# Feed-forward units of a split-precision decoder kernel: from 512-column and 256-column matmuls to 256-column matmuls throughout

## What is computed

```python
def _swiglu(x, w_gate, w_up, w_down):
    return (jax.nn.silu(x @ w_gate) * (x @ w_up)) @ w_down

for l in range(DEPTH):                      # DEPTH = 2
    x = _layer_norm(DN_ALPHA * x + 0.5 * _swiglu(x, ffn1...), ln1_g[l], ln1_b[l])
    x = _layer_norm(DN_ALPHA * x + _hybrid_mixer(x, ...), ln2_g[l], ln2_b[l])
    x = _layer_norm(DN_ALPHA * x + 0.5 * _swiglu(x, ffn2...), ln3_g[l], ln3_b[l])
```

## Time and profile before

| | |
|---|---|
| median of 3 runs | 1286.24 us (1286.09 to 1286.31) |
| the profiled execution's own time | 1286.24 us |
| its span | 1283.9 us |
| TensorE (PE) busy | 1272.0 us, 99% |
| PE weight loads (PEld) busy | 1143.4 us, 89% |
| DVE busy | 911.8 us, 71% |
| ACT busy | 642.0 us, 50% |
| granted TensorE clock, mean | 0.999 |

### The profile page before, as it was taken

One profiled execution on the slowest core, in us unless ns is written; L12 is line 12 of the kernel. 1 busy time (PEld: TensorE's weight loads), 2 busy tenths in 40 slices (PEclk: granted clock), 3 DMA queues, 4 the chain that ended last, 5 costly groups with the idle time before them and its releaser, 6 DMA issues.

```text
span 1283.9 us, 18456 instructions
## 1 busy us (share of the span) xinstructions
PE 1272.0 (99%) x7905; PEld 1143.4 (89%) x7905; DVE 911.8 (71%) x1106; ACT 642.0 (50%) x662; POOL 68.8 (5%) x59
## 2 busy tenths in 40 slices
PE   8999999999999999999999999999999999999997
PEld 7888889998999988888888888899989998888886
DVE  6566669898675787665686666799977756866665
ACT  5444445694544354444454444466836454544441
POOL 0299000000000000000000000000000000000000
PEclk9999999999999999999999999999999999999999
DMA  8855647643666556566566655466436765665551
GB/s 299 263 187 193 197 134 226 198 134 99 197 197 199 196 186 213 192 197 196 164 197 229 193 185 189 155 198 197 131 99 197 229 193 170 197 229 187 186 187 64
DMA packets 177841, 240.04 MB, mean 187 GB/s; under 512 B 8224, under 2 KB 147104, under 8 KB 177632
## 3 DMA queue, kind: packets, MB, share of 16 engines
q1 hardware_dynamic: 177376, 237.03, 57.5%
q0 software_dynamic: 240, 1.71, 0.4%
q10 hardware_dynamic: 144, 0.13, 0.1%
HBM read 237.80 MB, written 1.05 MB: 186 GB/s over the span
## 4 chain that ended last, share of the span: by engine, by line
PE 98%; DVE 1%; ACT 1%; DMA 0%; DVEq 0%; issue 0%
PE ps L1536 22%; PE ps L1511 22%; PE ps L1519 11%; PE ps L1439 11%; PE ps L1437 11%; PE ps L1438 11%; PE ps L1502 5%; PE ps L1459 1%; PE ps L1726 1%; PE ps L1685 0%; PE ps L1686 0%; ACT rot_sw L647 0%; PE ps L1712 0%; PE ps L1713 0%; PE ps L1711 0%; PE ps L1727 0%
## 5 line engine op out<-in xcount | busy, mean ns | idle before, releaser
L859 DVE TENSOR_TENSOR wlo<-raw,whi 128x2048 fp32r<-128x2048 f32 (+1 forms) x218 | 492.4, 2276 | 188.5 <-ACT whi L561 188.4
L561 ACT ACTIVATE whi<-raw 128x2048 fp32r<-128x2048 f32 (+1 forms) x218 | 413.1, 1898 | 276.6 <-DMA raw<-w_in 108.5
L1511 PE MATMUL ps<-xpair,whi 128*128 128x512 f32 x1216 | 290.0, 390 | 0.0
L1511 PEld LDWEIGHTS ps<-xpair,whi 128*128 128x128 f32 x1216 | 225.7, 188 | 45.2
L1437 PE MATMUL ps<-xpair,whi 128*128 128x256 f32 x800 | 224.3, 280 | 0.0
L1439 PE MATMUL ps<-xpair,wlo 128*128 128x256 f32 x800 | 222.7, 278 | 0.0
L1438 PE MATMUL ps<-xpair,whi 128*128 128x256 f32 x800 | 222.7, 278 | 0.0
L1519 PEld LDWEIGHTS ps<-xpair,wlo 128*128 128x128 f32 x1216 | 154.5, 189 | 6.1
L1519 PE MATMUL ps<-xpair,wlo 128*128 128x256 f32 x1216 | 156.4, 281 | 0.0
L1438 PEld LDWEIGHTS ps<-xpair,whi 128*128 128x128 f32 x800 | 150.6, 188 | 0.4
L1437 PEld LDWEIGHTS ps<-xpair,whi 128*128 128x128 f32 x800 | 150.2, 188 | 0.4
(11 more groups left out here) (238 smaller groups left out, 1604.1 us busy)
## 6 DMA issues: line engine op xcount, KB each, us to landing
raw<-w_in SPq DMA_DIRECT2D x60, 1024.0 KB, 5.2
raw<-ffn_w_down SPq DMA_DIRECT2D x44, 1024.0 KB, 4.9
raw<-ffn_w_gate SPq DMA_DIRECT2D x40, 1024.0 KB, 5.4
raw<-ffn_w_up SPq DMA_DIRECT2D x40, 1024.0 KB, 5.4
raw<-w_br SPq DMA_DIRECT2D x12, 1024.0 KB, 5.0
raw<-w_out SPq DMA_DIRECT2D x8, 1024.0 KB, 4.8
g_row<-ln_rows SPq DMA_DIRECT2D x6, 512.0 KB, 6.4
b_row<-ln_rows SPq DMA_DIRECT2D x6, 512.0 KB, 7.2
```

Source lines behind the costliest of these rows:

```text
L561: act.activation(unit(whi, n), unit(raw, n), ACT.Copy).then_inc(w_hi, 1)
L859: dve.tensor_tensor(w_low(n), unit(raw, n), unit(whi, n).bitcast(F32), ALU.subtract).then_inc(w_lo, 1)
L1511: pe.matmul(ps[:, bank, :], wh[:, kk, cols], xpair[:, kk, :, :], start=kk == 0, stop=kk == KC - 1, skip_group_check=True)
```

## The change

Gate and up units are made of 256-column matmuls alone. `high_pass` does, for each of the two 128-feature chunks and each of 8 blocks, whi·xhi and whi·xlo into the same 256 columns of one bank; `low_pass` adds wlo·xhi. A unit is 32 + 16 = 48 matmuls and one bank. Gate units take banks 6 and 7 by turns, up units 4 and 5. The two partial sums are gone, and with them the copies on ACT, the adds on DVE, `gsum`, `usum` and four semaphores: the silu and the product read PSUM directly. PE waits for the silu and the product of two steps earlier before it writes a bank again. The down units of j = 1 to 9 (`narrow_rows`) stream each 512 columns of weights as two matmuls of 256, both from the same stationary block. In the up unit of j = 1 one plain fp32 matmul, `ones` with `xf`, is added behind the four transposes; its output is overwritten by what follows.

```diff
-            def gate_of(j):
                 act.wait_ge(w_used, done_no(base + 3 * j - 1))
...
-                act.activation(silu[:, :], gsum[:, :], ACT.Silu).then_inc(silu_done, 1)
+                act.activation(silu[:, :], ps[:, gate_bank(j), :], ACT.Silu).then_inc(silu_done, 1)
...
-        def wide_part(bank, n):
+        def high_pass(bank, n):
             wh = slot(n, FB)[0]
-            cols = slice((bank % 2) * P, (bank % 2 + 1) * P)
-            for kk in range(KC):
-                pe.matmul(ps[:, bank, :], wh[:, kk, cols], xpair[:, kk, :, :],
-                          start=kk == 0, stop=kk == KC - 1, skip_group_check=True)
+            for c in range(2):
+                out, cols = ps[:, bank, c * SEQ:(c + 1) * SEQ], slice(c * P, (c + 1) * P)
+                for kk in range(KC):
+                    pe.matmul(out, wh[:, kk, cols], xhi[:, kk, :], start=c == kk == 0, stop=False, skip_group_check=True)
+                    pe.matmul(out, wh[:, kk, cols], xlo[:, kk, :], start=False, stop=False, skip_group_check=True)
...
-        def low_part(bank, n):
+        def low_pass(bank, n):
             wl = slot(n, FB)[1]
...
+            for c in range(2):
+                out, cols = ps[:, bank, c * SEQ:(c + 1) * SEQ], slice(c * P, (c + 1) * P)
+                for kk in range(KC):
+                    last = pe.matmul(out, wl[:, kk, cols], xhi[:, kk, :], start=False, stop=kk == KC - 1,
+                                     skip_group_check=True)
...
+        def narrow_rows(n, t, pick):
+            wh, wl = slot(n, D_MODEL)
+            for bank in (2 * t, 2 * t + 1):
+                for kk in range(2):
+                    t_hi, t_lo = pick(kk, t)
+                    for i, (x, w) in enumerate(((t_hi, wh), (t_hi, wl), (t_lo, wh))):
+                        for c in range(2):
+                            lo_c = 512 * (bank % 2) + SEQ * c
+                            last = pe.matmul(ps[:, bank, c * SEQ:(c + 1) * SEQ], x, w[:, kk, lo_c:lo_c + SEQ],
+                                             start=False, stop=i == 2, skip_group_check=True)
...
-                if j > 1:
-                    pe.wait_ge(gate_summed, gate_no(l, w, j - 1))
-                else:
-                    pe.wait_ge(tok_hid, tile_no(nth, 0))
-                paired(FFN_GATE, gate).then_inc(w_used, 1)
+                if j > 2:
+                    pe.wait_ge(silu_done, gate_no(l, w, j - 2))
+                high_pass(gate_bank(j), gate)
+                pe.wait_ge(w_lo, done_no(gate))
+                low_pass(gate_bank(j), gate).then_inc(w_used, 1)
...
+                    pe.matmul(ps[:, up_bank(j), 0:SEQ], ones, xf[:, 0, :], start=True, stop=True)
+                elif j > 2:
+                    pe.wait_ge(prod_done, gate_no(l, w, j - 2))
+                high_pass(up_bank(j), up)
...
-                tile_rows(down, 0, pick)
+                if j < NF - 1:
+                    narrow_rows(down, 0, pick)
+                else:
+                    tile_rows(down, 0, pick)
```

More of the change, by code:

```diff
@@ L161, in build @@
     hlo_last = place("hlo_last", [P, 2 * SEQ], F32R, r_u2 + 10240)
-    gsum = place("gsum", [P, 2 * SEQ], F32, r_u2 + 12288)
-    usum = place("usum", [P, 2 * SEQ], F32, r_u2 + 14336)
     PADW = SEQ + CONV - 1
@@ L352, in gate_no, with gate_bank, up_bank @@
         return nth_ffn(l, w) * (NF - 1) + j
-    def up_no(l, w, j):
-        return nth_ffn(l, w) * (NF - 2) + j
+    def gate_bank(j):
+        return FFN_GATE + j % 2
+    def up_bank(j):
+        return FFN_UP + (j - 1) % 2
     def tile_no(stage, t):
@@ L573, in tile_silu, with silu_of @@
                 act.activation(silu[:, t * SEQ:(t + 1) * SEQ], ps[:, TILE_BANK[t], 0:SEQ], ACT.Silu).then_inc(tok_silu, 1)
-            def gate_of(j):
+            def silu_of(j):
                 act.wait_ge(w_used, done_no(base + 3 * j - 1))
-                if j > 1:
[L579 to L584, removed]
                 if j > 1:
@@ L588, in silu_of @@
                     act.wait_ge(tok_hid, tile_no(nth, 1))
-                act.activation(silu[:, :], gsum[:, :], ACT.Silu).then_inc(silu_done, 1)
-            def up_of(j):
-                act.wait_ge(w_used, done_no(base + 3 * j))
-                act.activation(halves(usum[:, :]), ps[:, FFN_UP:FFN_UP + 2, SEQ:], ACT.Copy).then_inc(up_part, 1)
+                act.activation(silu[:, :], ps[:, gate_bank(j), :], ACT.Silu).then_inc(silu_done, 1)
             if nth:
@@ L603, in ffn @@
                 hi(base + 3 * j + 2)
-                gate_of(j)
                 silu_of(j)
@@ L877, in tile_split @@
                 dve.tensor_tensor(hlo[:, :], ps[:, FFN_UP + 1, :], hhi[:, :].bitcast(F32), ALU.subtract).then_inc(hid_lo, 1)
[L879 to L883, removed]
             def product(j):
[L887 to L892, removed]
-                else:
-                    dve.wait_ge(w_used, done_no(base + 3 * j))
-                    up = ps[:, FFN_UP, :]
+                dve.wait_ge(w_used, done_no(base + 3 * j))
                 dve.wait_ge(silu_done, gate_no(l, w, j))
                 dve.wait_ge(hid_lo, step_no(l, w, j - 1))
-                dve.scalar_tensor_tensor(out=hid[:, :], in0=up, scalar=0.5 / ALPHA, in1=silu[:, :],
+                dve.scalar_tensor_tensor(out=hid[:, :], in0=ps[:, up_bank(j), :], scalar=0.5 / ALPHA, in1=silu[:, :],
                                          op0=ALU.mult, op1=ALU.mult).then_inc(prod_done, 1)
@@ L1537, in tokens @@
                                  skip_group_check=True)
+            return last
+        def narrow_rows(n, t, pick):
[8 more added lines that the diff above has]
+                                             start=False, stop=i == 2, skip_group_check=True)
             return last
@@ L1630, in ffn @@
                     last.then_inc(hid_turned, 1)
[L1631 to L1643, removed]
+                    pe.matmul(ps[:, up_bank(j), 0:SEQ], ones, xf[:, 0, :], start=True, stop=True)
+                elif j > 2:
+                    pe.wait_ge(prod_done, gate_no(l, w, j - 2))
+                high_pass(up_bank(j), up)
+                pe.wait_ge(w_lo, done_no(up))
+                low_pass(up_bank(j), up).then_inc(w_used, 1)
                 pe.wait_ge(w_lo, done_no(down))
@@ L1652, in ffn @@
                 if j < NF - 1:
-                    tile_rows(down, 1, pick).then_inc(w_used, 1)
+                    narrow_rows(down, 1, pick).then_inc(w_used, 1)
             pe.wait_ge(w_lo, done_no(down + 1))
```

16 lines of the change are left out of this document (removed).

## The result

| | before | after |
|---|---|---|
| median of 4 runs | 1286.21 us | 1313.05 us (1312.93 to 1313.32) |
| the profiled execution's own time | 1286.24 us | 1313.02 us |
| its span | 1283.9 us | 1310.7 us |

The ratio is 1.0208 (95% interval 1.0196 to 1.0220): 26.8 us slower. The prediction was 1280.4 us with a range up to 1306; the time lies outside it, on the other side, and even above the case of slow pace everywhere.

What follows compares the result with a forecast made beforehand. PE, busy 99% of the span, was taken as the bound, an FFN's time being its matmul steps. Gate, up and down terms summed to -1.44 us per FFN, -5.8 for four: 1286.2 - 5.8 = 1280.4 us, range 1279 to 1306.

Steps and rivals of the forecast that it cites:

- case of slow pace everywhere: All four FFNs stay at 117.9 ns a 256-column step: +18.8 us, 1305.0 us in all.
- I take the quick end: FFN 256-column matmuls: of the bounds 113.4 and 117.9 ns a step, it chose 113.4; chance of this case 0.53.
- The bounds 113.4 and 117.9: Quick and slow ns a step of 256-column matmuls, read from `features` in the mixer, taken as limits for the FFNs.
- The fp32 matmul sets the quick pace: In each FFN, the added matmul brings 113.4 ns a step until j = 10: -1.44 us, for four FFNs -5.8.
- 0.44 us each: Forecast cost of each added fp32 matmul, 0.25 + 0.30 - 0.11 us; four cost 1.8 us.
- Rival 1: The fp32 matmul doesn't set the pace, all four FFNs slow: 1286.2 + 18.8 = 1305.0 us; chance 0.25.
- gate 1: Gate unit of j = 1 in each FFN, slow behind 512-column matmuls: 5.66 against 5.51 us, +0.15.
- up 1: Up unit of j = 1, with transposes and fp32 matmul: 6.34 us if quick (+0.33), 6.53 if slow (+0.52).
- Rival 3: Each added matmul costs 0 to 8.8 ns everywhere; at the middle, with the fp32 ones, 1297.2 us; chance 0.05.
- ACT, DVE and DMA at nothing, no new wait of PE: Removing 76 ACT copies and 76 DVE adds costed at nothing, DMA unchanged; a new PE wait had chance under 0.01.
- Once quick, it was quick until the next plain fp32 or 512-column matmul: Read from the mixer before: the 113.4 ns pace held until such a matmul, at longest some 620 matmuls.
- the 5.8 us that I had expected of the whole change: Forecast gain over four FFNs at the quick pace, -1.44 us each: 1286.2 - 5.8 = 1280.4 us.

Runs made afterwards that it cites:

- a1: The changed kernel without the added fp32 matmul in the up unit of j = 1; 1311.63 us, ratio 1.0196 to the kernel before.
- a2: The changed kernel with `xpair` begun 64 bytes earlier; 1307.82 us, ratio 1.0166 to the kernel before.
- a3: As a2, with `hhi`, `hlo` and the last pair of hidden features also begun 64 bytes later; 1303.10 us, ratio 1.0130.
- a4: The changed kernel with FFN units, from the third to the ring's last full turn, begun 2 x SHIFT into their slots and hidden features 128 bytes later; 1292.79 us.
- b1: a4 with its down units in 512-column matmuls again and `hhi`, `hlo` at distance 0 from the weights; 1298.12 us, ratio 1.0092.
- b3: The changed kernel with `xpair` 192 bytes earlier and `hhi`, `hlo` 128 bytes later, run once; 1320.09 us.
- b4: The kernel before with only the down units of j = 1 to 9 in 256-column halves, `hhi`, `hlo` 64 bytes later; 1294.86 us, ratio 1.0074.
- c1: b1 with `hhi`, `hlo` where they were, no fp32 matmul, and slots moved up to the end of each FFN; 1282.42 us, ratio 0.9972.
- b2: a4 without the added fp32 matmul; 1290.80 us, ratio 1.0039 to the kernel before.
- c2: c1 with the slots of the first two units of each FFN moved too; 1281.27 us, ratio 0.9965 to the kernel before.
- c4: The changed kernel with 512-column matmuls in all down units and no address moved; 1302.78 us, ratio 1.0130 to the kernel before.

## Why the prediction was wrong

In one table, what the kernels showed of a 256-column step in the FFNs. H is `high_pass`, L `low_pass`, D the down units of j = 1 to 9; the number is the distance, then ns a step (median of the units, from the first to the last start in each). Where units fall into two paces, both stand there with the number of units; an up unit of j = 1 counts by the pace at its end.

| kernel | H | L | D | us |
|---|---|---|---|---|
| after, a1 | 0: 120.0 | 1: 117.8 | 0: 120.0 | 1313.05, 1311.63 |
| a2 | 1: 114 (76), 118 (4) | 2: 118.2 | 0: 119.9 | 1307.82 |
| a3 | 1: 114 (44), 118 (36) | 2: 118.2 | 1: 114 (32), 118 (4) | 1303.10 |
| a4 | 1: 114 (61), 118 (13); 0: 120 (6) | 1: 113 (61), 118 (19) | 1: 114 (3), 118 (31); 2: 118.5 (2) | 1292.79 |
| b1 | 1: 118 (73), quick (1); 0: 120 (6) | 1: 118 (79), 113 (1) | 0, wide: 226.7 | 1298.12 |
| b3 | 3: 113 (19), 118 (61) | 0: 120.0 | 2: 119.9 | 1320.09 |
| b4 | 0, wide: 228.5 | 1: 117.8 | 1: 117.8 | 1294.86 |
| c1 | 1: 114 (73), 118 (7) | 1: 113 (73), 118 (7) | 3, wide: 228.8 (33), 233 (3) | 1282.42 |

- **"I take the quick end, because the same pairs of operands at 512 columns run at 227 with nothing lost ... the FFN's addresses are the better ones"**: this step failed, and it is the cause. What 512 columns show of an address doesn't carry to 256. Distance 0 costs nothing at 512 columns (226.7 in b1) and is the worst there is at 256 (120.0). The mixer's `2 * SHIFT`, which I read as the poorer place from the earlier trace rows, is distance 3 for wide matmuls there, and distance 1 for `features`: the very reason why could be quick. a2 and a4 showed it by moving either operand: `high_pass`, with its code as it was, left 120.0 for 114 in most units, and with all three kinds of unit at distance 1 the time fell by 20.3 us of the 26.8.
- **The bounds 113.4 and 117.9** were too narrow. The earlier trace rows all have distance 1, and the earlier trace rows the mixture of 0, 0 and 1 described above, so no row showed 256-column matmuls that were all at distance 0. With 120.0 for the 4288 matmuls of `high_pass` and `narrow_rows`, the all-slow sum of 1305.0 grows by 4288 x 2.1 ns = 9.0 us to 1314.0, against 1313.05.
- **The fp32 matmul sets the quick pace**: wrong in the FFNs. At distance 0 it can't (after); at distance 1 the up unit behind it is quick in one FFN of four, with it (a4) and without (b2). Its cost, 0.44 us each, lies between what the medians show (1.4 us for four in a1, 2.0 in b2).
- **Rival 1** was right in its sign and its two closest terms (gate 1 5.72 for 5.66, up 1 6.58 for 6.53), but for another reason. It had no third pace.
- **Rival 3** came nearest to the look of it, but a4, b4 and c2 refute a fixed charge for each matmul: c2 has 1216 more of them than the kernel before and takes 5 us less.
- **ACT, DVE and DMA at nothing, no new wait of PE**: right, by PE's waits after.
- **"Once quick, it was quick until the next plain fp32 or 512-column matmul"**: right for the rows of before, but not a rule. In a4 quick ends at a down unit that has neither ahead. b1 and c1 add that what comes behind 512-column matmuls depends on the distance at which these ran: behind 0 slow stays, behind 3 quick comes at the fifth or sixth matmul.

What is shown is the third pace: it comes and goes with the distance, with either operand moved. What stays open is which of the two others is entered at distance 1: why the down units of a4 are slow while most of a3's are quick (they are entered from different paces of `low_pass`, and no run separated that), why the same stretch of the mixer was quick in one trace and slow in another, and what in the hardware has a period of 256 bytes; only the moves of 64, 128 and 192 bytes were tried.

## What to carry to other kernels

When PE is the bound and its steps differ by a few per cent for one shape, read the step from start to start and the recorded length in each stretch, and ask for each stretch how far the stationary block starts from the moving operand, before asking what instruction stands ahead. A pace seen in one FFN or in one trace isn't yet the kernel's: count it in all of them. A price read from one shape or one pair of places isn't a bound for another: state which distance it was measured at. Splitting wide matmuls is free only where the narrow ones run at exactly half the wide step; moving slots by 64 and hidden features by 128 bytes was worth more here (20.3 us, a4) than the 5.8 us that I had expected of the whole change.

## What the hardware showed that I had not expected

- For fp32r matmuls of 256 columns the step was 120.0 ns where all of them were at distance 0 (after), 113.3 or 117.8 at 1 (a4) and at 3 (b3), and 118.1 to 119.9 at 2 (a2, b3), with a granted clock of 0.998 to 1.0, the upper level.
- At 512 columns the order is the other way round: 226.7 ns at distance 0; at 3 228.8, or 233 where a slow unit stood ahead (c1); 232 to 233 at 1 and 2 (the last down units of b1, a4 and b3).
- A pace outlives what set it: slow lasted two units (96 matmuls) behind the wide matmuls of b1, with addresses that ran quick in a4. And it can differ from one trace to another with the same mixer code, addresses and instructions just ahead: 623 matmuls at 117.8 in c4, at 113.3 in the others (2.2 us of a 1305 us execution).
